# Block 2's gate tiles as one 512-column matmul into half banks, added up by VectorE

## The reference

```
def second_block(x, ...):
    for i in range(DEPTH):                       # 2 layers
        x = x + 0.5 * swiglu(rms_norm_2(x, ffn1_norm[i]), ...)
        h = rms_norm_2(x, mix_norm[i])
        proj = h @ w_in[i]
        z, xbc, dt_raw, q, k, v = jnp.split(proj, splits, axis=-1)
        xbc = jax.nn.silu(causal_depthwise_conv(xbc, conv_w[i], conv_b[i]))
        y_ssd = ssd_mixer(xbc, dt_raw, z, ...)   # scan; y * silu(z), norm by group
        y_att = dilated_attention(q, k, v)       # 16 heads of 64
        x = x + jnp.concatenate([y_ssd, y_att], axis=-1) @ w_out[i]
        x = x + 0.5 * swiglu(rms_norm_2(x, ffn2_norm[i]), ...)
```

## Time and profile before

| | |
|---|---|
| Timed runs | 1897.56 us median of 3 (1897.54 to 1897.67) |
| Profiled execution, span | 1896.0 us |
| Median less span | 1.56 us |
| TensorE busy, share of the span | 100% |
| VectorE busy | 77% |
| ScalarE busy | 62% |
| GpSimd busy | 21% |
| Granted TensorE clock, mean | 1.000 |

### The profile page before, as it was taken

How to read it: one execution, slowest core, us unless ns; L and a number is a source line. 1 busy time by engine, 2 the same in 40 slices (tenths; PEclk the granted TensorE clock), 3 DMA queues, 4 the chain that set the end, 5 groups by cost and what they waited for, 6 DMA issues and landing times.

```text
span 1896.0 us, 29617 instructions
## 1 busy us (share of the span) xinstructions
PE 1887.7 (100%) x11184; PEld 1631.0 (86%) x11184; DVE 1459.0 (77%) x2602; ACT 1174.4 (62%) x2167; POOL 396.1 (21%) x448
## 2 busy tenths in 40 slices
PE   9999999999999999999999999999999999999999
PEld 8789988887898888888988788888888898878887
DVE  6877996687799769866787978857885687897874
ACT  6667775567678556545667565545554667756552
POOL 1210211011011005411022214402440102223430
PEclk9999999999999999999999999999999999999999
DMA  9344566543455656565552355555565544345663
GB/s 368 123 134 142 197 202 226 167 156 120 136 190 190 209 169 204 190 195 179 175 167 93 122 186 190 189 191 186 190 190 191 188 156 152 104 143 181 190 194 127
DMA packets 91117, 331.96 MB, mean 175 GB/s; under 512 B 10080, under 2 KB 10592, under 8 KB 90592
## 3 DMA queue, kind: packets, MB, share of 16 engines
q1 hardware_dynamic: 90976, 330.08, 53.1%
HBM read 328.99 MB, written 1.05 MB: 174 GB/s over the span
## 4 chain that ended last, share of the span: by engine, by line
PE 90%; DVE 5%; ACT 3%; DMA 1%; issue 1%; SPq 0%; DVEq 0%; ACTq 0%
PE PS L83 87%; PE PS L86 3%; DVE WL L98 2%; DVE TMP L108 1%; ACT TMP L95 1%; ACT WH L92 1%; DVE SM L114 1%; DMA RAW<-wts 1%; DMA TMP<-xt 0%; DVE TMP L98 0%; ACT TMP L92 0%; DVE SM L108 0%; ACT M L92 0%; DVE GX L108 0%; DVE SM L98 0%
## 5 line engine op out<-in xcount | busy, mean ns | idle before, releaser
L98 DVE TENSOR_TENSOR WL<-RAW,WH 128x1024 fp32r<-128x1024 f32 (+1 forms) x610 | 760.8, 1253 | 285.1 <-ACT WH L92 281.6
L92 ACT ACTIVATE WH<-RAW 128x1024 fp32r<-128x1024 f32 (+1 forms) x610 | 640.1, 1053 | 313.1 <-PE PS L83 307.6
L83 PE MATMUL PS<-HX,WH 128*128 128x512 f32 (+1 forms) x1920 | 523.4, 344 | 0.9 <-DVE WL L98 0.3
L83 PE MATMUL PS<-WH,GX 128*128 128x512 f32 (+1 forms) x1636 | 523.5, 391 | 0.0
L83 PE MATMUL PS<-HX,WL 128*128 128x256 f32 x1488 | 414.0, 281 | 0.0
L83 PE MATMUL PS<-GX,WH 128*128 128x256 f32 (+1 forms) x1776 | 409.5, 330 | 0.4
L83 PEld LDWEIGHTS PS<-HX,WH 128*128 128x128 f32 x1920 | 330.9, 189 | 47.8 <-DVE TMP L108 1.1
L83 PEld LDWEIGHTS PS<-WH,GX 128*128 128x128 f32 x1636 | 306.2, 188 | 63.0 <-issue 2.4
L83 PEld LDWEIGHTS PS<-GX,WH 128*128 128x128 f32 x1776 | 298.0, 190 | 30.5 <-DVE TMP L108 1.2
L83 PE MATMUL PS<-WL,GX 128*128 128x512 f32 (+1 forms) x818 | 317.0, 388 | 0.0
L98 POOL TENSOR_TENSOR TMP<-TMP,RB 128x256 f32<-128x256 f32 x176 | 205.6, 1173 | 474.3 <-DVE TMP L98 235.0
(11 more groups left out here) (146 smaller groups left out, 1699.6 us busy)
## 6 DMA issues: line engine op xcount, KB each, us to landing
RAW<-wts SPq DMA_DIRECT2D x607, 512.0 KB, 4.5
M<-bias SPq DMA_DIRECT2D x4, 512.0 KB, 12.5
M<-bias SPq DMA_DIRECT2D x1, 2048.0 KB, 10.7
X<-x SPq DMA_DIRECT2D x2, 512.0 KB, 10.8
M<-mem SPq DMA_DIRECT2D x1, 1024.0 KB, 13.2
M<-memt SPq DMA_DIRECT2D x1, 1024.0 KB, 12.2
CST<-cst SPq DMA_DIRECT2D x1, 794.0 KB, 12.6
out<-X SPq DMA_DIRECT2D x3, 256.0 KB, 4.5
```

The source lines that it names most:

```text
L83: return Issued(self.eng and self.eng.matmul(o, l, r, start=first, stop=last, skip_group_check=share))
L92: return Issued(self.eng.activation(o, i, f, scale=scale))
L98: return Issued(self.eng and self.eng.tensor_tensor(o, a, b, op))
```

## The change

In both layers of block 2:

- TensorE makes the z tiles with `fm_halves`.
- ScalarE's new `z_rest(m)` copies columns 256 to 511 of the bank to `z_t(m)`, one step behind the tile. Its `z_tanh(m)` now reads the sum in SBUF and runs two steps behind.
- VectorE's new `z_join(m)` adds columns 0 to 255 of the bank to `z_t(m)`, one step behind; it is what frees the bank. `z_end(m)` now reads both inputs from SBUF and runs three steps behind.
- The last tanh and the last `z_end` are moved to behind the first weight half of `wa`, by `late`.
- The six places of `band_t` become three pairs, and `z_rest(m)` waits for `z_end(m-3)`.

```
+        def z_t(m):
+            return band_t(m % 3 * 2)
+        def z_tanh_t(m):
+            return band_t(m % 3 * 2 + 1)
...
-                        fm_tile(("z", L, m), whole, WT if m >= 2 else (0, 1))
+                        fm_halves(("z", L, m), whole, halves_of(1 - side), WT if m >= 2 else (0, 1))
...
+                def z_rest(m):
+                    key = ("z", L, m)
+                    if m >= 3:
+                        e.wait_ge(dout, ("z end", L, m - 3))
+                    e.wait_ge(tile, key)
+                    e.act(ACT.Copy, z_t(m), bank(key)[:, S:2 * S]).then_inc(aout, key)
+
                 def z_tanh(m):
-                    key = ("z", L, m)
-                    if m >= 6:
-                        e.wait_ge(dout, ("z", L, m - 6))
-                    e.wait_ge(tile, key)
-                    e.act(ACT.Tanh, band_t(m), bank(key)[:, 0:S], scale=0.5).then_inc(ready, ("zt", L, m))
+                    e.wait_ge(joined, ("z", L, m))
+                    e.act(ACT.Tanh, z_tanh_t(m), z_t(m), scale=0.5).then_inc(ready, ("zt", L, m))
...
                         highs(("z", L, m))
                         if m >= 1:
-                            z_tanh(m - 1)
+                            z_rest(m - 1)
+                        if m >= 2:
+                            z_tanh(m - 2)
                         yield
-                    z_tanh(7)
-                    yield from residual(("wa", L), 8)
+                    z_rest(7)
+                    z_tanh(6)
+                    yield from residual(("wa", L), 8, late={0: lambda: z_tanh(7)})
...
                 def z_end(m):
-                    key = ("z", L, m)
                     e.wait_ge(scored, (("dil", L), 2 * m + 1))
                     e.wait_ge(ready, ("zt", L, m))
-                    e.stt(Z[:, m, :], band_t(m), 1.0, bank(key)[:, 0:S], ALU.add, ALU.mult).then_inc(dout, key)
+                    e.stt(Z[:, m, :], z_tanh_t(m), 1.0, z_t(m), ALU.add, ALU.mult).then_inc(dout, ("z end", L, m))
+
+                def z_join(m):
+                    key = ("z", L, m)
+                    e.wait_ge(aout, key)
+                    e.tt(z_t(m), z_t(m), bank(key)[:, 0:S], ALU.add).then_inc(joined, key)
...
                         lows(("z", L, m))
-                        if 2 <= m < 7:
-                            z_end(m - 2)
-                        if m >= 6:
-                            z_end(m - 1)
+                        if m >= 1:
+                            z_join(m - 1)
+                        if m >= 3:
+                            z_end(m - 3)
                         yield
-                    z_end(7)
-                    yield from residual(("wa", L), 8, behind=True, hold=True)
+                    z_join(7)
+                    z_end(5)
+                    z_end(6)
+                    yield from residual(("wa", L), 8, behind=True, hold=True, late={0: lambda: z_end(7)})
```

More of the change, by code:

```diff
@@ L2711, in pool_program @@
                     y = XC[:, m, :]
-                    e.wait_ge(dout, ("z", L, m))
+                    e.wait_ge(dout, ("z end", L, m))
                     e.wait_ge(dout, ("y", L, m))
```

## The result

The changed kernel takes 1901.53 us (median of 15 runs, 1901.23 to 1901.85) against 1897.53 us before in the same series: a ratio of 1.0021, 95% interval 1.0014 to 1.0028. It is slower by 4.0 us, and the interval lies to both sides of the 0.2% that the prediction took as the limit of what can be told. The forecast was 1901.2 us. The span grew from 1896.0 to 1899.8 us, by 3.8 us.

The account below looks back on a forecast made before the run. TensorE was taken to bound except where the chain passes through VectorE and ScalarE. There +0.49 and +1.32 us a layer, twice, gave +3.6: span 1899.6, timed 1901.2 us; own range 1900.2 to 1902.2, 80% range 1898.4 to 1904.0.

Parts of the forecast that it names:

- TensorE's part: Gate tiles: pairs 0.347 us apart replace triples of 0.360, saving 0.86 us a layer, spent in waiting.
- The attention loop: Last attention steps: added VectorE and ScalarE instructions delay probs(14) 0.96 us, tile 5 0.60, the last weighing 0.49.
- The scan: VectorE's scan: four more instructions of 0.33 us add 1.32, putting masks of heads 4 and 5 1.81 us late.
- GpSimd: Scan: the 0.49 us lost beside GpSimd's product moves from the WL subtraction to z_end(5), costing nothing more.
- The late tanh: Scan, ScalarE: it waits for z_join(7), delaying exps of heads 4 and 5 some 1.5 us; costed at nothing.
- The sum: Both layers: 0.49 in attention plus 1.32 in scan, +1.81 us a layer, +3.6 in all; span 1899.6, time 1901.2.
- The first: Transpose bank wait: TensorE remains the bound and keeps its gain, 3.1 us faster, 1894.4 us; chance 0.06.
- The second: Scan or loop: slack absorbs one's lag, leaving +0.5 to +1.3 us a layer, about 1899.4 us; chance 0.22.
- the third: Scan: late exps reach TensorE or GpSimd meets two instructions, +2.0 to +4.0 us over the sum; chance 0.17.
- The fourth: Whole kernel: the additions hide wholly and the waits stay, 1.7 us less, 1895.9 us; chance 0.05.

Follow-up runs that it names:

- e1_halves_only: Kernel before with only TensorE's z tiles changed to fm_halves, columns 256 to 511 left out of the result; 1897.3 us, ratio 0.9999.
- e2_adds_only: Changed kernel with the old matmuls (fm_tile), all added copies and additions kept, so the gate is doubled; 1901.75 us, ratio 1.0022.
- e7_no_tanh: Changed kernel without ScalarE's tanh, z_end taking the sum twice; 1901.05 us, ratio 1.0018.
- e3_in_gap: Changed kernel with VectorE's attention z_join and z_end moved into its idle time before the second reciprocal, z_end one step earlier in the scan; 1898.61 us.
- e4_old_tail: Changed kernel with z tiles 5 to 7, whose work falls into the scan, made in the old form; 1899.62 us, ratio 1.0011.
- e9_before_in_gap_one_less: Kernel before with z_end(0) to z_end(3) in VectorE's idle time of steps 5 to 8, z_end(4) in that at the attention's end; 1896.08 us.
- e10_gpsimd_apart: Kernel before with one added GpSimd wait, moving its product of y and the gate beside VectorE's PSUM-reading decay; 1897.08 us, ratio 0.9996.
- e8_gpsimd_ends: e3_in_gap with z_end(3) to z_end(7) given to GpSimd as a product and a sum; 1899.24 us, ratio 1.0009.

## Why the prediction was right

All distances are from the anchor, less those of before.

- **TensorE's part.** 0.347 us a pair was foreseen. It is measured in tiles 2, 3 and 5 of the changed kernel in layer 0; in the others a pair takes 0.349 to 0.354 us, so the eight tiles saved about 0.6 us a layer and not 0.86. That the saving would be spent in waiting is shown by e1_halves_only (no gain) and e2_adds_only (no less cost without it).
- **The attention loop.** Foreseen: the exps of heads 14 and 15 +0.66, `probs(14)` +0.96, tile 5 +0.60, the weighing +0.49. Measured: +0.69, +0.99, +0.62 (39.16 against 38.54) and +0.50. The tanh's 0.30 in it is 0.28 by e7_no_tanh. e3_in_gap takes the whole of it away, and with it more.
- **The scan.** Foreseen: VectorE takes up +0.49 and is +1.81 at the masks of heads 4 and 5. Measured: +0.50 and +1.84. Three of the four instructions are priced by e4_old_tail (1.00 on VectorE), a single one by e9_before_in_gap_one_less (0.33).
- **GpSimd.** The loss of 0.49 us was to move from the subtraction to `z_end`. The subtraction now takes 1.21 us, and two `z_end` 1.17 in place of 0.66: 0.51. *SBUF — State Buffer* of the Trainium skill has an exclusive lock for this ("SBUF: two separate sides"), which these rows and those of e10_gpsimd_apart agree with; e8_gpsimd_ends shows the loss at full size.
- **The late tanh.** It waits 1.05 us, the exps of heads 4 and 5 behind it, and the masks that want them come about 1 us after the last of these exps (1057.63 with 0.41, masks at 1059.02). Costed at nothing, and nothing by the chain.
- **The sum.** +1.81 a layer foreseen, +1.84 and +1.85 measured; 1899.6 for the span against 1899.8. Of the error of 0.3 us in time, 0.07 is in the stretch, and 0.17 is the median's distance to the span, 1.73 us here and 1.56 before; the small rest is span outside the stretch.
- **The rivals.** The first (TensorE keeps its gain) falls with e1_halves_only and with the waits of 0.37 and 0.60 us in TensorE's timeline. The second (half of it absorbed) would show as idle time on VectorE behind 1046.74: there is none up to the masks. Of the third, only 0.03 us a layer is there. The fourth falls with e2_adds_only.

**What the prediction had not seen.** Two waits that cost nothing here. TensorE's weighing of the pair before the last waits 0.37 us at 1039.36 for VectorE's `low`, which reads the bank that the weighing writes; it disappears in the later wait for `probs(14)`. And `z_rest(7)` waits 1.08 us at 1053.81 for `z_end(4)`, by the ring of three pairs. The chances of the prediction put 0.58 on no difference and 0.40 on slower; the ratio of 1.0021 fell 0.0001 to the slower side of that line.

## What to carry to other kernels

A busy line of 99% doesn't say that the engine bounds every stretch: a change that takes work from TensorE and gives it to VectorE is to be priced at the place where the chain leaves TensorE, instruction by instruction, and there 0.33 us of VectorE was 0.33 us of each layer. Before changing the form of the work, look for idle time of the lagging engine that the written order doesn't use: one hook into a gap took 0.42 us a layer off the old kernel, and, with one instruction fewer in the scan, 1.55 off the new form. When GpSimd works beside VectorE, try its instructions next to those that read PSUM; here a single added wait gave 0.49 us a layer back to VectorE.

## What was unexpected of the hardware

- In these rows, who starts first keeps its time. In the kernel before, GpSimd's first product starts at 1055.64 and VectorE's subtraction at 1055.74; the product takes 0.74 us and the subtraction 1.71. At the next meeting VectorE's subtraction is first. VectorE's timeline and GpSimd's, both of the kernel before:

```profile
1059.74 1.21 DVE L98 TENSOR_TENSOR WL<-RAW,WH 128x1024 fp32r<-128x1024 f32 x1
```

```profile
1059.90 2.60 POOL L98 TENSOR_TENSOR M<-M 128x256 f32<-128x256 f32 x1 [3.52 <-DVE M L108]
```

  The subtraction keeps its 1.21 us, and the product lasts 2.60, until the masks behind the subtraction, also with two inputs in SBUF, are through. In e10_gpsimd_apart this product lasts 0.73 us beside `decay`. The prediction had read only the first meeting.
- Small pieces add up: in e8_gpsimd_ends, the additions and products that GpSimd does instead of VectorE, ten in each layer, cost VectorE 0.5 us more than they took off it.
- A matmul with its weight load left out, at equal columns, was worth 13 ns where the pairs stand 0.347 us apart (0.360 for three), and only about 6 in tiles 6 and 7 of the changed kernel, where they stand 0.353 and 0.354 apart. Next to none of it reached the end time where VectorE was late.
